# RWKV's triangular inverse: 64x64 diagonal blocks packed side by side, quadrant products instead of full 128x128 ones

## What is computed

```python
def rwkv7_scan(r, decay, k, v, kk, a):
    def step(state, inp):
        r_t, w_t, k_t, v_t, kk_t, a_t = inp
        sa = jnp.einsum('bhvk,bhk->bhv', state, -kk_t)
        state = (state * w_t[:, :, None, :]
                 + sa[..., None] * (kk_t * a_t)[:, :, None, :]
                 + v_t[..., None] * k_t[:, :, None, :])
        return state, jnp.einsum('bhvk,bhk->bhv', state, r_t)
```

## Time and profile before

| | |
|---|---|
| time, median of 3 runs | 1449.54 us (1448.19 to 1452.68) |
| the profiled execution | 1452.29 us, its span 1450.5 us |
| PE busy | 1226.9 us, 85% of the span |
| DVE, ACT busy | 608.2 us (42%), 442.2 us (30%) |
| mean granted TensorE clock | 0.934 of full speed |
| chain that ended last | PE 61%, DMA 21%, DVE 7% |
| the inverse, from the first turn to the first product with values | 147.1 to 217.1 us of the span |

### The profile page before, as it was taken

How to read it: one execution, slowest core, us unless ns; L and a number is a source line. 1 busy time by engine, 2 the same in 40 slices (tenths; PEclk the granted TensorE clock), 3 DMA queues, 4 the chain that set the end, 5 groups by cost and what they waited for, 6 DMA issues and landing times.

```text
span 1450.5 us, 17980 instructions
## 1 busy us (share of the span) xinstructions
PE 1226.9 (85%) x7610; PEld 896.4 (62%) x7610; DVE 608.2 (42%) x964; ACT 442.2 (30%) x684; POOL 16.1 (1%) x32
## 2 busy tenths in 40 slices
PE   5999999999999998999999989898564665636677
PEld 5998886599887786599988776654321322312222
DVE  4688432476643657366642548822100101101001
ACT  4652430343433685353432523532010000000001
POOL 3000000000000000000000000000000000000000
PEclk9999999999999999999999999998786878878889
DMA  8352569454564554155554634069999999999994
GB/s 267 127 205 87 177 210 331 162 174 175 185 214 152 196 191 158 58 174 175 176 210 165 202 103 147 1 275 408 430 427 428 428 427 429 429 428 427 430 427 192
DMA packets 98349, 362.98 MB, mean 250 GB/s; under 512 B 7226, under 2 KB 10645, under 8 KB 86373
## 3 DMA queue, kind: packets, MB, share of 16 engines
q1 hardware_dynamic: 96240, 357.70, 63.8%
q0 software_dynamic: 1680, 4.10, 1.0%
q10 hardware_dynamic: 356, 0.13, 0.1%
HBM read 360.87 MB, written 1.05 MB: 250 GB/s over the span
## 4 chain that ended last, share of the span: by engine, by line
PE 61%; DMA 21%; DVE 7%; ACT 2%; issue 1%; SPq 1%; DVEq 0%; ACTq 0%
PE bank L911 32%; DMA arena<-in_exp_w 20%; PE bank L619 7%; PE bank L1025 3%; PE bank L850 2%; PE bank L1534 2%; DVE arena L2182 2%; PE bank L883 2%; PE bank L1218 2%; PE bank L1245 2%; PE bank L696 2%; PE bank L1237 1%; PE bank L893 1%; SPq L2766 1%; DVE arena L2105 1%
## 5 line engine op out<-in xcount | busy, mean ns | idle before, releaser
L619 PE MATMUL bank<-arena 128*32 128x512 f32 x880 | 188.8, 690 | 74.7 <-DMA arena<-in_exp_w 73.7
L1697 DVE TENSOR_TENSOR low_w<-ring,split_high 128x2048 fp32r<-128x2048 f32 x84 | 189.7, 2288 | 103.3 <-ACT split_high L2376 103.3
L911 PE MATMUL bank<-turned_high,low_w 128*128 128x256 f32 x720 | 204.6, 284 | 0.0
L2376 ACT ACTIVATE split_high<-ring 128x2048 fp32r<-128x2048 f32 x84 | 157.8, 1916 | 138.1 <-DMA ring<-in_w_down 66.3
L619 PE MATMUL bank<-ring,arena 128*32 128x512 f32 x528 | 96.4, 709 | 82.3 <-DMA arena<-in_exp_w 82.3
L911 PE MATMUL bank<-turned_high,split_high 128*128 128x256 f32 x512 | 145.8, 285 | 3.0 <-DVE turned_low L1712 3.0
L911 PE MATMUL bank<-turned_low,split_high 128*128 128x256 f32 x512 | 144.9, 283 | 0.0
L911 PEld LDWEIGHTS bank<-turned_high,low_w 128*128 128x128 f32 x720 | 139.1, 193 | 0.0
L619 PEld LDWEIGHTS bank<-arena 128*32 128x32 f32 x880 | 50.7, 125 | 134.1 <-issue 131.7
L765 DVE TENSOR_TENSOR arena<-arena,bank 128x512 f32<-128x512 f32 x8 | 5.5, 688 | 295.9 <-PE bank L619 253.7
L2361 ACT ACTIVATE arena<-bank 128x512 f32<-128x512 f32 x110 | 62.2, 596 | 209.3 <-PE bank L911 135.8
(11 more groups left out here) (439 smaller groups left out, 1982.0 us busy)
## 6 DMA issues: line engine op xcount, KB each, us to landing
arena<-in_exp_w SPq DMA_DIRECT2D x59, 2048.0 KB, 23.2
ring<-in_exp_w SPq DMA_DIRECT2D x33, 2048.0 KB, 20.2
ring<-in_w_up SPq DMA_DIRECT2D x16, 2048.0 KB, 8.7
ring<-in_w_down SPq DMA_DIRECT2D x16, 2048.0 KB, 7.8
ring<-in_mod_w SPq DMA_DIRECT2D x12, 2048.0 KB, 8.4
ring<-in_w_in_ar SPq DMA_DIRECT2D x7, 2048.0 KB, 8.2
ring<-in_w_qkv SPq DMA_DIRECT2D x6, 2048.0 KB, 8.5
ring<-in_ple_gate SPq DMA_DIRECT2D x4, 2048.0 KB, 8.4
```

Source lines behind the costliest of these rows:

```text
L619: last = nc.tensor.matmul(mb[bank][strip(e), :], act[:, k, strip(e)], w[e][:, k, cols], start=(k == 0), stop=(k == n_k - 1), skip_group_ch ...
L911: last = mm(dst, *pair, start=(start and i == 0), stop=(stop and i == 2))
L1697: v.tensor_tensor(low_of(name, s), half_of(slot(name), name, s), high_of(name, s).bitcast(F32), ALU.subtract).then_inc(sem("split_low"), 1)
L2376: nc.scalar.activation(high_of(name, s), half_of(slot(name), name, s), ACT.Copy)\
```

## The change

The first six levels never leave the two 64x64 diagonal blocks. The new kernel keeps only those: `near_inv`, `near_invT` and `a_inv` hold for each of the 16 matrices the upper block in partitions 0 to 63 and the lower block in partitions 64 to 127, 64 columns wide. A product of 128x128 becomes two of 64x64, one on rows 0 to 63 and output partitions 0 to 63, one on rows and output partitions 64 to 127, issued in turn; both write the same columns of one bank. A turn becomes a float32 product with the identity, 64x64 again, two for each matrix. At level 64 only the corner block is wanted, and it takes 16 products of 64x64 for "ax" and 16 for "xax", all "ax" on one quadrant and all "xax" on another. The copies of ACT and DVE are 256 columns wide instead of 512. ACT copies five masks to a packed place (`near_masks`) before the copies of the first turn and, during level 64, spreads the two blocks into `invT`; DVE clears the other corner of `invT` after level 4. The new waits are those on `near_masks`, `inv_zero` and `inv_spread`.

```diff
--- before.py
+++ after.py
@@ -294,6 +294,10 @@
             i = LEVELS.index(m)
             return c_("level", i * P, (i + 1) * P)
 
+        def near_mask(m):
+            i = LEVELS.index(m) - 1
+            return near_masks[:, i, :]
+
         def v1(name, i, n=1):
             s = v1_at[name][0] + i
             return vec[:, s:s + n]
@@ -350,8 +354,10 @@
         w_sb, sa_sb = half(4), half(5)
         ab = page(19, 4).rearrange("p (i a s) -> p i a s", i=16, a=2)
         ak = page(23, 4).rearrange("p (i a s) -> p i a s", i=16, a=2)
-        inv, invT = blocks(page(16, 2), 16), blocks(page(8, 2), 16)
-        a_inv = blocks(xn[:, :], 16)
+        near_inv, near_invT, invT = blocks(page(8), 16), blocks(page(9), 16), blocks(page(16, 2), 16)
+        BLOCKS = [slice(0, 64), slice(64, 128)]
+        near_masks = xn[:, 1024:1024 + 64 * (len(LEVELS) - 2)].rearrange("p (m c) -> p m c", c=64)
+        a_inv = blocks(xn[:, 0:1024], 16)
         s1 = page(4)[:, 0:256].rearrange("p (j v) -> p j v", j=4)
 
         hq, hk, hf, hgT = (blocks(page(i), 4) for i in (12, 13, 14, 18))
@@ -1225,33 +1231,52 @@
                         read_by(mod_bank, "mod", c)
 
             pe.wait_ge(sem("inv_first"), 1)
-            for g in range(4):
-                bank = banks.take(pe, "x", 1, g)
-                transposes([(bank.ap[:, i * P:(i + 1) * P], invT[:, 4 * g + i, :]) for i in range(4)], bank)
+            def near_turn(m):
+                for g in range(4):
+                    if m > 1:
+                        banks.wait_read(pe, "xax", m, g)
+                    bank = banks.take(pe, "x", m, g)
+                    for i in range(4):
+                        for b in BLOCKS:
+                            last = mm(bank.ap[b, i * 64:(i + 1) * 64], near_invT[b, 4 * g + i, :], ident[b, b],
+                                      start=True, stop=True)
+                    last.then_inc(bank.full, 1)
+
+            near_turn(1)
             two_pairs("k", k_til)
             for n, m in enumerate(LEVELS[1:]):
                 for g in range(4):
                     banks.wait_read(pe, "x", LEVELS[n], g)
                     bank = banks.take(pe, "ax", m, g)
                     for i in range(4):
-                        last = mm(bank.ap[:, i * P:(i + 1) * P], ab[:, 4 * g + i, 0, :], inv[:, 4 * g + i, :],
-                                  start=True, stop=True)
+                        at = slice(i * 64, (i + 1) * 64)
+                        if m < 64:
+                            for b in BLOCKS:
+                                last = mm(bank.ap[b, at], ab[b, 4 * g + i, 0, b], near_inv[b, 4 * g + i, :],
+                                          start=True, stop=True)
+                        else:
+                            last = mm(bank.ap[BLOCKS[1], at], ab[BLOCKS[0], 4 * g + i, 0, BLOCKS[1]],
+                                      near_inv[BLOCKS[0], 4 * g + i, :], start=True, stop=True)
                     last.then_inc(bank.full, 1)
                 modulation(n)
                 for g in range(4):
                     banks.wait_read(pe, "ax", m, g)
                     bank = banks.take(pe, "xax", m, g)
                     for i in range(4):
-                        last = mm(bank.ap[:, i * P:(i + 1) * P], a_inv[:, 4 * g + i, :], invT[:, 4 * g + i, :],
-                                  start=True, stop=True)
+                        at = slice(i * 64, (i + 1) * 64)
+                        if m < 64:
+                            for b in BLOCKS:
+                                last = mm(bank.ap[b, at], a_inv[b, 4 * g + i, :], near_invT[b, 4 * g + i, :],
+                                          start=True, stop=True)
+                        else:
+                            last = mm(bank.ap[BLOCKS[0], at], a_inv[BLOCKS[1], 4 * g + i, :],
+                                      near_invT[BLOCKS[1], 4 * g + i, :], start=True, stop=True)
                     last.then_inc(bank.full, 1)
-                if m != LEVELS[-1]:
-                    for g in range(4):
-                        banks.wait_read(pe, "xax", m, g)
-                        bank = banks.take(pe, "x", m, g)
-                        transposes([(bank.ap[:, i * P:(i + 1) * P], invT[:, 4 * g + i, :]) for i in range(4)], bank)
+                if m < 64:
+                    near_turn(m)
                 if m == 4:
                     gated_turn()
+            pe.wait_ge(sem("inv_spread"), 2)
             for g in range(4):
                 banks.wait_read(pe, "xax", LEVELS[-1], g)
             def from_state(pair, t, a):
@@ -1902,7 +1927,9 @@
                 bank = banks.read(dve, "bonus", c)
                 v.tensor_tensor(page(11)[:, c * 512:(c + 1) * 512], bank.ap, page(4)[:, c * 512:(c + 1) * 512],
                                 ALU.mult).then_inc(bank.freed, 1)
-            step(v.tensor_copy(invT, mid(ident, 16)))
+            for b in BLOCKS:
+                last = v.tensor_copy(near_invT[b], mid(ident[b, b], 16))
+            step(last)
             both = const[:, cols_at["strict"][0]:cols_at["upto"][1]]
 
             def take_two_pairs(dst, tag):
@@ -1923,7 +1950,9 @@
                 banks.wait_read(dve, "pairs", i)
             for i in (8, 9, 12, 13):
                 banks.wait_read(dve, "pairs", "b", i)
-            v.copy_predicated(invT, mid(level_mask(1), 16).bitcast(I32), ab[:, :, 0, :]).then_inc(sem("inv_first"), 1)
+            for b in BLOCKS:
+                last = v.copy_predicated(near_invT[b], mid(level_mask(1)[b, b], 16).bitcast(I32), ab[b, :, 0, b])
+            last.then_inc(sem("inv_first"), 1)
             dve.wait_ge(sem("inv_first"), 1)
             banks.read(dve, "in", 3, 1)
             take_two_pairs(ak, "k")
@@ -1953,12 +1982,19 @@
             for m in LEVELS[1:]:
                 for g in range(4):
                     bank = banks.read(dve, "xax", m, g)
-                    v.copy_predicated(invT[:, 4 * g:4 * g + 4, :], mid(level_mask(m), 4).bitcast(I32),
-                                      blocks(bank.ap, 4)).then_inc(bank.freed, 1)
+                    if m == 2 and g == 0:
+                        dve.wait_ge(sem("near_masks"), 2)
+                    if m < 64:
+                        v.copy_predicated(near_invT[:, 4 * g:4 * g + 4, :], mid(near_mask(m), 4).bitcast(I32),
+                                          blocks(bank.ap[:, 0:256], 4)).then_inc(bank.freed, 1)
+                    else:
+                        v.tensor_copy(invT[0:64, 4 * g:4 * g + 4, 64:128], blocks(bank.ap[0:64, 0:256], 4))\
+                            .then_inc(bank.freed, 1)
                 if m == 2:
                     gated_norm()
                 elif m == 4:
                     gated_gate()
+                    v.memset(invT[64:128, :, 0:64], 0.0).then_inc(sem("inv_zero"), 1)
             def take_halves(dst, tag, t):
                 for half_ in range(2):
                     bank = banks.read(dve, tag, t, half_)
@@ -2500,16 +2536,25 @@
                     for b in range(2):
                         evacuate(bk_tok[:, b], ACT.Copy, "bk", b)
                 evacuate(hgT[:, 2 * i:2 * i + 2, :], ACT.Silu, "in", 3, i)
-            for g in range(4):
-                evacuate(inv[:, 4 * g:4 * g + 4, :], ACT.Copy, "x", 1, g)
+            def keep_quarter(dst, rows_, *name):
+                for g in range(4):
+                    bank = banks.read(act, *name, g)
+                    s.activation(dst[rows_, 4 * g:4 * g + 4, :], blocks(bank.ap[rows_, 0:256], 4), ACT.Copy)\
+                        .then_inc(bank.freed, 1)
+
+            for b in BLOCKS:
+                s.activation(near_masks[b], blocks(c_("level"), len(LEVELS))[b, 1:-1, b], ACT.Copy)\
+                    .then_inc(sem("near_masks"), 1)
+            keep_quarter(near_inv, slice(0, P), "x", 1)
             act.wait_ge(sem("hgrn_sq"), 1)
             s.activation(hg_ss, hg_ss, ACT.Sqrt).then_inc(sem("hgrn_root"), 1)
             for m in LEVELS[1:]:
-                for g in range(4):
-                    evacuate(a_inv[:, 4 * g:4 * g + 4, :], ACT.Copy, "ax", m, g)
-                if m != LEVELS[-1]:
-                    for g in range(4):
-                        evacuate(inv[:, 4 * g:4 * g + 4, :], ACT.Copy, "x", m, g)
+                keep_quarter(a_inv, slice(0, P) if m < 64 else BLOCKS[1], "ax", m)
+                if m < 64:
+                    keep_quarter(near_inv, slice(0, P), "x", m)
+            act.wait_ge(sem("inv_zero"), 1)
+            for b in BLOCKS:
+                s.activation(invT[b, :, b], near_invT[b], ACT.Copy).then_inc(sem("inv_spread"), 1)
             evacuate(mod_sum[:, :], ACT.Copy, "mod")
             act.wait_ge(sem("rwkv_sq"), 1)
             s.activation(rw_ss, rw_ss, ACT.Sqrt).then_inc(sem("rwkv_root"), 1)
```

## The result

The changed kernel takes **1442.5 us** (median of 19 runs, 1437.9 to 1448.8), the kernel before, measured beside it, 1452.2 us (19 runs): ratio 0.9933, interval 0.9923 to 0.9944. That is 9.7 us faster, where 19.3 were forecast. The direction was right, the time lies inside the range, and half of the gain is missing.

A forecast was written before the change was run, and what follows sets the result against it. PE's instructions were taken to bound the inverse. Gains of 16.2 (levels 2 to 32) and 3.7 us (level 64), less 0.15, 0.1, 0.2 and 0.1, gave 19.3 us: 1449.54 to 1430.2 us, range 1425 to 1445.

The forecast's parts named there:

- The price of a record: 64x64 products in the inverse: 0.059 us each on one tile, 0.0295 us with two quadrants in turn.
- Rival 2: Short records in the inverse have a floor, 0.044 us each: gain only 2.6 us, 1446.9 us; chance 0.10.
- The other price in the working: By the skill's rule for load-and-matmul pairs, 0.081 us a record per tile, 0.0405 on two: 1442.9 us.
- rival 1: Two quadrants writing one bank don't overlap, 0.059 us a record: slower by 10.9 us, 1460.4 us; chance 0.11.
- Level 64: Last level: 16 products each for ax and xax on one quadrant, plus a shorter DVE copy: gain 3.7 us.
- The copies: ACT and DVE copies in the level loop end before PE returns, with 0.4 us margin, so PE stays the bound.
- The masked copy ahead of the first turn: DVE's copy that PE waits on, split by partitions into two of 1024 columns: 2.75 us, costing 0.1 us.
- The 0.1 us charged for ACT at level 2: ACT's root ends late, so its first ax copy may hold up PE by up to 0.3 us; 0.1 taken.
- The stretches behind: Everything after the inverse starts earlier by the same amount and keeps its length.
- rival 4: The gain is not passed on because a later transfer doesn't move: 1449 us; chance 0.03.
- Modulation weights: Slots refilled three levels ahead, 23 us instead of 33, 2 MB a level at 272 GB/s: hidden, no cost.
- Rival 3: The clock falls to 1.2 GHz while quadrants are in use, through the whole inverse: 1476 us; chance 0.03.

The follow-up runs named there:

- e3: Kernel before, with level 64 alone done by 64x64 quadrants: 1449.0 us, ratio 0.9968.
- e1: Changed kernel, with modulation units 3 to 11 loading 64 weight columns instead of 4096, all PE instructions kept: 1432.2 us, ratio 0.9854.
- f1: Changed kernel, each modulation unit loaded in four 512 KB pieces, released one by one for units 3 to 7: 1439.9 us, ratio 0.9911.
- f2: Changed kernel, each modulation unit loaded in two 1 MB pieces, the second released at the end of the turn: 1439.6 us in one run.
- f3: Changed kernel, each modulation unit loaded in four 512 KB pieces without pauses between them: 1441.7 us in one run.
- g1: Changed kernel, with the turn behind level 32 made for the upper blocks only: 1442.3 us, ratio 0.9929.
- e2: Changed kernel without the turns of the lower blocks from level 2 on, 160 of 1208 records of each kind fewer: 1435.3 us in one run.
- h1: Changed kernel, with modulation units 3 to 11 loading half their weights, 1 MB each: 1436.6 us, ratio 0.9882.
- g2: Changed kernel, modulation units in two paced 1 MB pieces and the turn behind level 32 for upper blocks only: 1438.3 us, ratio 0.9892.

## Why the prediction was wrong, and what of it was right

**The price of a record: right.** 64 records of ax, xax or turn take 2.03 to 2.10 us where no stop falls into them, forecast 2.08; a level 7.68, forecast 7.70. One weight load takes 135 ns and one matmul 218. Rival 2, a floor for short records, has no room. Of the rows behind the price one was misread: L1106's weights are not contiguous, as the working says, but one column repeated 64 times (`to_broadcast`). The new loads, which are contiguous, take 135 ns all the same, so the value was right and one of its reasons not. The other price in the working, 0.0405 us a record and 1442.9 us in all, comes within 0.4 us of the measured time by coincidence: the records stand 0.0295 us apart, and the time was lost between them.

**Two row tiles in one bank: rival 1 is refuted.** 64 records in 2.08 us, where one quadrant alone does 32 in the same time (e3), are full overlap, both tiles writing the same bank. The Trainium skill's statement on page "TensorEngine Tiling (Array Packing)", section "Restrictions and Gotchas", that different row tiles cannot access the same bank at once, does not hold for this pair, the diagonal quadrants, which write different halves of the bank's partitions.

**Level 64: right**, 3.7 us forecast, 3.7 measured by e3.

**The copies: right.** Nearly the whole forecast rested on a margin of 0.4 us between a copy and PE's return. No wait of PE's matmuls in any level is put down to ACT or DVE. The masked copy ahead of the first turn takes 2 x 1.384 = 2.77 us, forecast 2.75. PE's wait behind level 64 fell by 0.2 us, forecast 0.3. The 0.1 us charged for ACT at level 2 did not show as idle time of PE.

**The stretches behind, and rival 4: right.** 31.8 and 251.0 us, as before; all that the inverse gained was passed on.

**The step that failed** is "Modulation weights. [...] Hidden", and with it the sentence in the first paragraph that the inverse costs what PE's instructions cost. The working asked only whether the *weights* would be in time, and they are: no wait in the inverse names them. It did not ask what else the queues bring: the supply of PE's instructions was put at nothing without a reason. Full 128x128 products spend 0.112 us on a record; alternating quadrants spend 0.0295. The change so doubles the number of instructions (1200 to 2416) while shortening the time, and the sum has a price for each instruction's execution but none for its supply. That absent term is 59.69 - 50.27 = **9.4 us** of the 19.3:

- 6.8 us are PE standing still: 7.91 us of idle time less e1's 1.12.
- 1.6 us come from the clock. Behind the 3 us stop, a stretch of 3.4 us has the lower level, 1.2 GHz:

```profile
182.50:185.90 3.40, 3.40 (x52) 2.48 (x51) 0.00 (x0) 1.15 (x3) 0.00 (x0) 0.50 0.04 13
185.90:189.30 3.40, 3.40 (x86) 2.30 (x80) 1.38 (x4) 0.00 (x0) 0.00 (x0) 1.00 0.25 45
```

  The 44 records of ax left over take 2.48 us there instead of 43 x 0.0295 + 0.218 = 1.49, and the modulation 2.49 instead of 1.92: 1.0 and 0.6 us. Five kernels have such a stretch in the inverse (after, f1, f2, f3, g1), and in each a stop of 1.9 to 3.0 us has ended at most 2.1 us ahead of it; e1, which has no stop over 0.3 us but the last, has none. But stops of 2.77 us in f3 (an earlier one), of 2.76 in e2 and of 2.48 in h1 and g2 were not followed by one so soon. So the stretch goes with a stop, without following from each; no run tests it further.
- The last 1.0 us is mostly the price of stopping in mid-run. The last record before a stop runs out for 0.218 us, where the next would have started after 0.03: five stops, 0.9 us by this estimate. h1, at full clock with its stops, is busy for 0.9 us more than e1 (50.05 to 49.18).

**Rival 3** had the clock wrong in size and cause. It fell for 3.4 us, not for the inverse, and behind a pause, not for quadrants: e1 runs all of it at 1.00.

**The range** was held by luck: it reached up to 1445 us for rival 2, which has no part in the result. The miss was in no case on the list.

**What stays open.** Why a block starts late while weights are in flight: behind packets in a DMA engine's queue, or behind something that the trace does not show. The packet itself takes the same time. In f1 to f3, cutting the transfers into pieces did not make the stops go away. Moving the modulation's weights out of the inverse altogether was not tried, because a ring of three slots of 2 MB has no room for them ahead of it.

## What to carry to other kernels

Before splitting big products into many small ones, count PE's instructions per microsecond beside what the instruction queue brings, and look at what the DMA engines carry then: here a block of instructions every 12 us cost nothing beside 2 MB bursts, and one every 4.6 us cost 9.4 us of 59.7. Idle time of PE that is put down to "issue", in the middle of a run and while ACT and DVE wait too, at places 256 instructions apart, is the sign; taking away the transfers in both kernels is the test. In such a kernel an instruction is worth removing even where its execution lies in another's shadow (e2, in one run), but where it stands matters, since only the stops at ends of blocks can give anything back.

## What the runs showed that was not expected

- The supply of instructions can bind PE: stops of 0.3 to 3.0 us, 7.0 us in sum, that lie 256 or 512 instructions apart, end 1.2 to 1.6 us behind the landing of a 16 KB block, and all but vanish (0.3 us) without the weights.
- The order of tiles matters in part only. Alternating quadrants, 64 records take 2.08 us; in runs of eight on each, 2.69 (one execution); on one quadrant they would take about 4.0 (63 x 0.06 + 0.22).
- A lateness outlives its cause: 2.48 us of standing still with the DMA engines at 0.04 (h1).
